# Residual added in PSUM during the expert search, and the expert weight ring reloaded by halves

## The reference, cut to what matters

```python
aff = softmax(h2 @ w_router)                     # 256 tokens x 16 experts
vals, idx = lax.top_k(aff.T, 32)                 # each expert takes its 32 best tokens
xs = h2[idx]                                     # 16 x 32 x 1024
y = (silu(xs @ w_gate) * (xs @ w_up)) @ w_down * vals     # 1024 -> 512 -> 1024
x = x + g_f * zeros.at[idx].add(y)               # back to the tokens' rows
out = rmsnorm(x, norm_final)
```

## Time and profile before

| | us |
|---|---|
| median of 3 runs (lowest, highest) | 679.66 (679.27, 682.19) |
| profiled execution, its own time | 679.7 |
| its span | 677.6 |
| PE busy | 589.6 (87%) |
| DVE busy | 288.5 (43%) |
| ACT busy | 217.5 (32%) |

### The profile page before, as it was taken

How to read it: one execution, slowest core, us unless ns; L and a number is a source line. 1 busy time by engine, 2 the same in 40 slices (tenths; PEclk the granted TensorE clock), 3 DMA queues, 4 the chain that set the end, 5 groups by cost and what they waited for, 6 DMA issues and landing times.

```text
span 677.6 us, 8686 instructions
## 1 busy us (share of the span) xinstructions
PE 589.6 (87%) x3453; PEld 374.9 (55%) x3453; DVE 288.5 (43%) x688; ACT 217.5 (32%) x475; POOL 41.9 (6%) x74
## 2 busy tenths in 40 slices
PE   6989999999998989999999999998999755667554
PEld 6978877778766767748755454457353310121111
DVE  3356576676666350466727877236220100010002
ACT  4245353455334331474426755121010100010001
POOL 3000000000000000100002443000000000000000
PEclk9999999999999998999999999999999898798879
DMA  8594767657688663656568103557899999999994
GB/s 340 191 357 178 302 249 266 264 212 271 260 332 344 242 262 125 249 214 227 196 263 308 66 1 125 231 187 327 340 429 426 428 428 426 427 423 430 428 419 169
DMA packets 19512, 192.48 MB, mean 284 GB/s; under 512 B 3472, under 2 KB 4752, under 8 KB 7696
## 3 DMA queue, kind: packets, MB, share of 16 engines
q1 hardware_dynamic: 16016, 188.49, 69.6%
q10 hardware_dynamic: 3168, 1.87, 1.0%
q0 software_dynamic: 288, 1.57, 0.6%
HBM read 190.35 MB, written 1.05 MB: 282 GB/s over the span
## 4 chain that ended last, share of the span: by engine, by line
PE 64%; DMA 23%; DVE 7%; ACT 3%; issue 2%; POOL 1%; ACTq 0%; SPq 0%; DVEq 0%; POOLq 0%
PE bank L1094 25%; DMA ring<-in_stream 21%; PE bank L1071 6%; PE bank L1082 5%; PE bank L1631 4%; PE bank L1368 3%; PE bank L1581 2%; PE bank L1133 2%; PE bank L1531 2%; PE bank L1499 2%; PE bank L1466 2%; PE bank L1567 2%; PE bank L1422 2%; DMA vvc<-vvc 1%; DVE weight_parts L1912 1%
## 5 line engine op out<-in xcount | busy, mean ns | idle before, releaser
L1094 PE MATMUL bank<-weight_parts,u_parts 128*128 128x512 f32 (+2 forms) x416 | 127.4, 389 | 2.7 <-ACT mo L710 1.1
L1912 DVE TENSOR_TENSOR weight_parts<-ring,weight_parts 128x1024 fp32r<-128x1024 f32 (+2 forms) x64 | 73.2, 1180 | 41.8 <-ACT weight_parts L710 40.0
L1094 PEld LDWEIGHTS bank<-weight_parts,u_parts 128*128 128x128 f32 x416 | 76.7, 191 | 20.8 <-issue 2.6
L710 ACT ACTIVATE weight_parts<-ring 128x1024 fp32r<-128x1024 f32 (+2 forms) x64 | 63.9, 1021 | 34.3 <-PE bank L1094 24.1
L1094 PE MATMUL bank<-weight_parts,x_parts 128*128 128x512 f32 (+1 forms) x128 | 48.4, 378 | 0.0
L1094 PE MATMUL bank<-u_parts,weight_parts 128*128 128x256 f32 x192 | 36.7, 288 | 2.5 <-DVE weight_parts L1912 2.4
L1038 POOL TENSOR_TENSOR small<-small 128x1 f32<-128x1 f32 (+1 forms) x14 | 8.3, 596 | 451.9 <-DVE small L2300 215.6
L774 ACT ACTIVATE sp<-sp,small 128x128 f32<-128x128 f32 (+1 forms) x48 | 21.3, 444 | 36.2 <-DVE small L1836 36.2
L1094 PEld LDWEIGHTS bank<-u_parts,weight_parts 128*128 128x128 f32 x192 | 30.4, 191 | 3.5 <-issue 2.5
L988 ACT ACTIVATE sp<-bank 128x512 f32<-128x512 f32 x4 | 2.4, 597 | 87.5 <-PE bank L1631 87.5
L1631 PE MATMUL bank<-ring,tz 128*32 128x512 f32 x112 | 18.4, 797 | 11.8 <-DMA ring<-in_stream 11.8
(11 more groups left out here) (316 smaller groups left out, 1071.0 us busy)
## 6 DMA issues: line engine op xcount, KB each, us to landing
ring<-in_stream SPq DMA_DIRECT2D x43, 2048.0 KB, 8.9
parts<-in_stream SPq DMA_DIRECT2D x12, 2048.0 KB, 33.5
qk<-in_stream SPq DMA_DIRECT2D x9, 2048.0 KB, 13.2
tabs<-in_stream SPq DMA_DIRECT2D x6, 2048.0 KB, 22.4
mo<-in_stream SPq DMA_DIRECT2D x5, 2048.0 KB, 29.5
vvc<-in_stream SPq DMA_DIRECT2D x5, 2048.0 KB, 32.7
tz<-in_stream SPq DMA_DIRECT2D x5, 1024.0 KB, 37.5
lat<-in_stream SPq DMA_DIRECT2D x5, 1024.0 KB, 39.6
```

The source lines that it names most:

```text
L710: ins = act.activation(dst, src, ACT.Copy, scale=scale)
L1094: ins = pe_.matmul(o, lhs(a, c, i), rhs(b, c, i), start=(c == 0 and n == 0), stop=(c == chunks - 1 and n == 2))
L1912: dve.tensor_tensor(quarter(weight_parts[:, SLOT:], name, q), quarter(slot(name), name, q), quarter(weight_parts, name, q).bitcast(F32), A ...
```

## The change

The residual's four products move from group 0 of the expert loop to the search on DVE, in place of most of the `unread` transposes. `x_sb` is then free, and holds the first half of D0.2. From there on every slot is loaded by halves: the host puts its columns in the order that makes the first half the first 512 columns or the first chunk of all four experts, and each of the 18 half buffers is loaded again when PE has used that half (`h_used`). For group 3, all left halves of D come ahead of all right halves, and the last right half comes in two quarters. The gather of group 0 has a bank for each chunk, DVE and ACT take turns to copy them out, and only the first four chunks stand ahead of G0.0. norm_final is spread in group 1 instead of group 0. At the end the left half of the output is scattered and squared ahead of the right one, with `unread` transposes between the last slots' products; the last right half goes through DVE and the scatter in two quarters of 256 columns, and ACT scales two of the four half rows.

```diff
-WARM = {"ou11": 28, "rT11": 10, "ls1": 8, "afT": 8}
+WARM = {"ou11": 28, "rT11": 10, "ls1": 8}
+WHOLE = 10
+HALVES = ([(name, h) for name in STREAM[N_DENSE + WHOLE:-4] for h in range(2)]
+          + [(f"D{NG - 1}.{i}", h) for h in range(2) for i in range(4)])
+UNITS_IN_RING = 2 * len(EXPERT_CYCLE)
-TAIL = ["ou00", "ou01", "ou10", "rT00", "rT01", "ou11", "rT10", "rT11", "lg1", "ls1", "afT", "slT", "gx0", "gx1"]
+TAIL = ["ou00", "ou01", "ou10", "rT00", "rT01", "ou11", "rT10", "rT11", "lg1", "ls1", "afT", "slT", "gx0", "gx1", "gx2", "gx3",
+        "gx4", "gx5", "gx6", "gx7"]
...
+          **{f"gx{c}": (2, 7, 1)[c % 3] for c in range(KC)}}
...
+        def half_columns(name, half, a, b):
+            if (name, half) not in HALVES:
+                return slot_columns(name, SLOT // 2 * half + a, SLOT // 2 * half + b)
+            k = HALVES.index((name, half))
+            if k == 0:
+                return x_sb[:, a:b]
+            i, h = divmod((k - 1) % UNITS_IN_RING, 2)
+            return slot_columns(STREAM[N_DENSE + i], SLOT // 2 * h + a, SLOT // 2 * h + b)
...
         @block.sync
-            for n, name in enumerate(STREAM):
+            for n, name in enumerate(STREAM[:N_DENSE + WHOLE]):
...
+            for k, (name, h) in enumerate(HALVES):
+                n = STREAM.index(name)
+                if k == 0:
+                    eng.wait_ge(x_added, 1)
+                else:
+                    eng.wait_ge(h_used, k if k <= UNITS_IN_RING else 2 * WHOLE + k - UNITS_IN_RING + 1)
+                w = SLOT // 4 if k == len(HALVES) - 1 else SLOT // 2
+                eng.dma_start(half_columns(name, h, 0, w), stream[n, :, SLOT // 2 * h:SLOT // 2 * h + w])\
+                   .then_inc(half_in(name, h)[0], 16)
+            eng.dma_start(half_columns(name, h, w, 2 * w), stream[n, :, SLOT // 2 + w:]).then_inc(last_quarter, 16)
...
         @block.scalar
+            for t in range(TOK):
+                eng.wait_ge(times_norm, t + 1)
+                eng.wait_ge(roots, 13 + t)
+                act.activation(xn[:, t, 0:512], xn[:, t, 0:512], ACT.Copy, scale=rs[:, 4 + t:5 + t]).then_inc(y_first, 1)
...
         @block.tensor
                 elif name == "slT":
-                    for i in range(CAP // 8):
-                        eng.wait_ge(top_found, i + 1)
-                        unread(WARM["afT"] * (1 + i // 3), bank[3])
+                    eng.wait_ge(x2_ready, 2 * TOK)
+                    for t in range(TOK):
+                        for h in range(2):
+                            ins = pe_.matmul(bank[4 + 2 * t + h][:, :], ident[:, :], xn[:, t, 512 * h:512 * h + 512],
+                                             start=True, stop=False)
+                    ins.then_inc(x_added, 1)
+                    eng.wait_ge(top_found, CAP // 8)
+                    unread(18, bank[3])
...
-            for name in TAIL:
+            for name in TAIL[:-4]:
...
+                        if (g, m) == (0, "G"):
+                            if i in (1, 2):
+                                tail(f"gx{2 * i + 2}")
+                                tail(f"gx{2 * i + 3}")
+                            kept(eng, f"gx{2 * i}")
+                            kept(eng, f"gx{2 * i + 1}")
                         for k in range(2):
+                            half_arrived(eng, f"{m}{g}.{i}", k)
...
-                        ins.then_inc(e_used, 1)
+                            ins.then_inc(h_used, 1)
...
+            g = NG - 1
+            for i in range(4):
+                half_arrived(eng, f"D{g}.{i}", 0)
+                for e in range(EG):
+                    ins = second_products(bank[2], e, i, 0, 0, 512)
+                if i == 3:
+                    ins.then_inc(e_first, 1)
+                unread(9, bank[0])
+            for i in range(4):
+                half_arrived(eng, f"D{g}.{i}", 1)
+                for q, where in ((0, bank[3]), (1, bank[1])):
+                    if (i, q) == (3, 1):
+                        eng.wait_ge(last_quarter, 16)
+                    for e in range(EG):
+                        ins = second_products(where, e, i, 1, 256 * q, 256)
+                    if i == 3:
+                        ins.then_inc(e_quarter, 1)
+                if i == 0:
+                    eng.wait_ge(e_y, NG)
+                    for t in range(TOK):
+                        scattered(g, t, 0).then_inc(e_out, 1)
+                elif i < 3:
+                    unread(9, bank[0])
+            for t in range(TOK):
+                for q in range(2):
+                    if t == 0:
+                        eng.wait_ge(e_y2, NG + q)
+                    ins = scattered(g, t, 1, 256 * q, 256)
+                ins.then_inc(e_out, 1)
...
         @block.vector
-            final_mean(0)
-            eng.wait_ge(roots, n_mean[0] + 1)
-            final_rows(0, 0)
...
+                dve.tensor_tensor(xn[:, t, 0:512], bank[4 + 2 * t][:, :], nfin[:, 0:512], ALU.mult).then_inc(times_norm, 1)
+            for q, where in ((0, bank[3]), (1, bank[1])):
+                a = 256 * q
+                eng.wait_ge(e_quarter, q + 1)
+                dve.tensor_tensor(yE[:, 512 + a:768 + a], where[:, a:a + 256], gF[:, 512 + a:768 + a], ALU.mult)\
+                   .then_inc(e_y2, 1)
+            for t in range(TOK):
+                final_mean(t)
+            for t in range(TOK):
+                eng.wait_ge(roots, n_mean[0] + t + 1)
+                dve.scalar_tensor_tensor(xn[:, t, 512:1024], bank[5 + 2 * t][:, :], rs[:, 4 + t:5 + t], nfin[:, 512:1024],
+                                         ALU.mult, ALU.mult).then_inc(y_ready, 1)
```

More of the change, by code:

```diff
@@ L566, in released @@
                 eng.wait_ge(mod_used, int(name[1:]) + 1)
-            else:
-                group, part = name[1:].split(".")
-                eng.wait_ge(e_used, 12 * int(group) + 4 * "GUD".index(name[0]) + int(part) + 1)
         def experts_done(eng, stage, g):
-            released(eng, f"{stage}{g}.3")
+            eng.wait_ge(h_used, 24 * g + 8 * "GUD".index(stage) + 8)
         def leave(ins, name):
@@ L669, in _ @@
                         filled(eng, "lg1")
[L670 to L676, removed]
+                    eng.dma_start(piece, stream[n, :, i:at]).then_inc(slot_in[b], 16)
                 if name == "W2":
@@ L978, in _ @@
                     soft(1)
-                elif name == "gx0":
+                elif name[:2] == "gx" and int(name[2]) % 2:
                     filled(eng, name)
-                    leave(chosen(D_(name), 0), name)
+                    c = int(name[2])
+                    leave(act.activation(xs[:, c, :], D_(name)[:, 0:P], ACT.Identity,
+                                         bias=mc[:, 0, 24 + c:25 + c], scale=scl[:, 2, c:c + 1]), name)
             for g in range(NG):
@@ L999, in _ @@
                 copy(hT, bank[0][:, :], scale=0.5).then_inc(e_hT, 1)
[L1000 to L1004, removed]
+                if g < 2:
+                    eng.wait_ge(gate_turn, g + 1)
+                    copy((gF, nfin)[g][:, 0:512], bank[0][:, :]).then_inc(gate_a, 1)
             for n, (h, t) in enumerate((h, t) for h in range(2) for t in range(TOK)):
@@ L1556, in tail, with gather @@
                     done(ins, name)
-                elif name in ("gx0", "gx1"):
-                    eng.wait_ge(oh_ready, 1)
+                elif name[:2] == "gx":
+                    if name == "gx0":
+                        eng.wait_ge(oh_ready, 1)
                     begin(name)
[L1560 to L1565, removed]
+                    done(gather(D_(name), 0, [int(name[2])]), name)
+            def gather(o, g, chunks):
+                for i, c in enumerate(chunks):
                     for t in range(TOK):
@@ L1650, in _ @@
                     for i in range(2):
-                        ins = gather(bank[2 + i], g + 1, i)
+                        ins = gather(bank[2 + i], g + 1, range(4 * i, 4 * i + 4))
                     ins.then_inc(side_turn, 1)
@@ L1675, in _ @@
[L1675 to L1681 removed]
+                        ins.then_inc(h_used, 1)
+                    if g < 2 and i == 1:
+                        row = (mc[:, 0, 40:48], nfc)[g]
+                        for c in range(KC):
+                            ins = pe_.matmul(bank[c // 4][:, c % 4 * P:c % 4 * P + P], row[:, c:c + 1].to_broadcast([P, P]),
+                                             ident[:, :], start=True, stop=True)
@@ L1692, in _ @@
-                for h in range(2):
-                    eng.wait_ge((e_y, e_y2)[h], g + 1)
-                    for t in range(TOK):
-                        ins = pe_.matmul(bank[4 + 2 * t + h][:, :], ohT[:, g, t * P:(t + 1) * P],
-                                         yE[:, 512 * h:512 * h + 512], start=False, stop=(g == NG - 1))
-                        if g == NG - 1 or (h, t) == (1, TOK - 1):
-                            ins.then_inc(e_out, 1)
+                            ins = scattered(g, t, h)
```

130 lines of the change are left out of this document (71 added, 59 removed).

## The result

The changed kernel takes 675.49 us (median of 14 executions), the kernel before 682.2 (also of 14): a ratio of 0.9933, with a 95% interval from 0.9915 to 0.9951. So it is faster, by 3.1 to 4.6 us by the ratios, where 7.1 were predicted: 44 to 65% of the forecast gain, with the 675.5 inside the range. The two medians lie 6.7 us apart, but that this is near the forecast is luck: five executions of the kernel before stood at 678.8 to 679.7 and nine at 681.3 to 683.2, and in the second comparison the medians lie 2.7 apart. The changed kernel's executions spread from 674.2 to 678.8. The profiled one took 678.64 (span 676.8), so it is one of the slow end, and that turned out to be the useful thing about it.

A forecast was written before the change was run, and what follows sets the result against it. The weight stream was taken to bound the kernel: restart at 473.45, plus 190.8, -2.45, +1.1 and -0.3 gave the last landing at 662.6; 7.85 for the end and 2.1 over the span gave 672.6 us, range 669.5 to 677.

The forecast's parts named there:

- What bounds the kernel: From 478 to 666 us the weight stream sets the time; its restart, bytes, rate and the work after it count.
- (a): After the dip near 470 us, the first reload of ring goes out at 473.45 instead of 475.94, 2.5 us earlier.
- (b): Half a slot loaded into x_sb during the dip leaves 2.45 us less of stream behind the restart.
- R2: Rival: the half in x_sb brings nothing, as the dip only moves; 675.1 us, chance 0.07.
- (c): In the stream, 34 additional loads cost 1.1 us in all, and finer rows gain 0.3 on the last slot.
- the 418 row: Lowest stream rate of three earlier stretches, 418 GB/s, giving an upper bound of 0.13 us per additional load, 4.4 in all.
- the last slot: At the stream's end, rows of 8 and 4 KB instead of 2 KB take off 0.3 us of a 0.5 us cost.
- R1: Rival: the stream's rate suffers, each additional load costing 0.13 us, in all 4.4; 675.9 us, chance 0.15.
- (d): Behind the last landing, the end takes 7.85 us, 3.0 less, as only a quarter is left to do.
- the 9 transposes behind each piece of D3: Between the last slots' products, 1.12 us with a quad's 0.87 at full clock stays under 2.45 between landings.
- R4: Rival: PE at 1.2 GHz misses the last landings and is about 11 us late; 685.3 us, chance 0.06.
- PE has no idle time before its last loads: Sign at the stream's end that, if seen, would show the forecast to be wrong.

The follow-up runs named there:

- e7: The changed kernel without the transposes in D3 and with nothing loaded into x_sb: 677.09 us, ratio 0.9952 to the kernel before.
- e8: The changed kernel without transposes in D3, nothing in x_sb, and one load per single-buffer slot up to U3.3: 675.5 us, ratio 0.9932 to the kernel before.
- e9: The changed kernel without transposes in D3, with 22 pairs of halves as single loads from the ring's second turn: 673.11 us, ratio 0.9892 to the kernel before.
- e6: The changed kernel without the six batches of transposes in D3, run a second time in another group: 674.65 us, ratio 0.992 to the kernel before.
- e1: The changed kernel without the six batches of nine warming transposes between D3's products: 674.68 us, ratio 0.9914 to the kernel before.
- e10: The changed kernel without transposes in D3, left output halves stored from ACT's queue, right ones from SP's: 675.24 us, ratio 0.9926 to the kernel before.
- e5: The changed kernel itself, measured again in a second comparison: 677.29 us, ratio 0.9955 to the kernel before.
- e4: The changed kernel, transposes kept, nothing in x_sb, and one load per single-buffer slot up to U3.3: 680.3 us, ratio 0.9991 to the kernel before.
- e3: The changed kernel, transposes kept, with nothing loaded into x_sb: 677.45 us, ratio 0.9964 to the kernel before.

## Why the prediction was right or wrong, step by step

**What bounds the kernel** was read rightly: everything that moved the restart, the bytes or the rate moved the end by as much, once PE was on time (e7, e8, e9).

**(a) The restart** came as worked out: 473.45 predicted, 474.06 with 0.6 of delay that was there at the load into tz, ahead of the change. From that load on, the gain is 14.94 - 12.44 = 2.50 us. **(b) The half in x_sb** was worth 2.50 (2.45 predicted), and R2 is refuted by e7.

**(c) The rate was mis-sized.** I took 1.1 us for all additional loads, a quarter of the bound by the 418 row. Measured: from e6 to the kernel before the stretch is 0.37 shorter, with a half of 2.50 left out of it and 0.3 estimated for the last slot, so halves cost 2.4 us (the 0.3 is still the prediction's estimate, no run measured it); e8 says 0.075 and e9 0.09 a slot. The rows that I read held this too weakly: one slot of nine in halves moves a mean of 44 us by 0.1. R1's direction was right, at half its price. Nor did SP's issues cost 0.33 each, as the prediction had it: with many loads queued, single ones held SP for up to 6.30 us in the changed kernel.

```profile
624.39 6.30 SPq L724 DMA_DIRECT2D tz<-in_stream  x1
```

That was hidden all the same: loads issued from 500 to 600 landed 26 to 30 us behind their issue (medians by buffer), and the stream never paused.

**(d) The end was mis-sized.** Behind the landing the engines did what was worked out: squares at L+1.9, the second mean at L+3.5, rows until L+5.1 (5.25 predicted), all in e1. The stores then took 3.7 us instead of 2.6, as all four are ready within 0.8 us and share the transfer (e10), so 8.8 instead of 7.85 and 2.1 us gained instead of 3.0.

**The step that failed** is the one that costs the transposes at nothing: "the 9 transposes behind each piece of D3 cost 1.12 us at full clock, a quad 0.87, together less than 2.45". The slack of 0.35 us at full clock was right. That it covers the transposes was not, for three reasons that the traces show. D3 begins 2.2 us behind its first landing (649.14 against 646.9), which I hadn't worked out at all. The clock is low then: the first half takes 3.98 us (649.14 to 653.12) and the second 3.08, against 2.48. And the first right half carries the scatter as well (2.92). The seven steps from 649.14 to 667.64 take 18.5 us against 17.4 between seven landings. With the 2.2 of the start and 0.43 for the first quarter's pass, which stands ahead of the last quarter's, that makes PE some 3.7 us late. I had the mechanism as R4, but only in its extreme form, at 1.2 GHz all through and 11 us late, with a chance of 6%. Its counter, that PE 80% busy stood at 1.00 from 454 on, didn't hold there: from 640 to 660 PE was busy 17.25 us of 20 at a mean of 0.62. And the prediction named the sign, "PE has no idle time before its last loads", which is what the profile shows. In the profiled execution the last quarter's pass could have begun by about 664.5 (474.06 + 190.45, the stretch of e1 and e6), and it began 0.43 behind 667.64, at 668.1: 3.6 us late. Leaving the batches out brings the waits for loads back (e1, e6) and takes 2.6 us off the median (e5 to e6).

By the Trainium skill (page "TensorE: Matmul & The Clock Gate", section "HAM oscillation — how this bites in real kernels") products that wait for loads start at the low clock again and again. The traces agree: means of 0.62 to 0.83 in the changed kernel's windows from 600 to 660, and the eight passes that start behind a wait at 641.97, and those at 644.46, take 1.93 us, where eight take 1.07 at full clock.

By the Trainium skill (page "DMA: Bandwidth & Descriptors", section "Anatomy of one DMA — SWDGE (gpsimd) path") a DMA has a fixed cost of some 2.0 us, an estimated 68 us for 34 more loads. That section is on DMAs issued by GpSimd, and these are SP's; for loads queued behind each other the runs disagree with the rule as it was used, with 2.4 us for all of them.

The sum with measured terms: -2.5 restart, -2.5 half, +2.4 rate, -0.3 last slot, -2.1 end, +2.6 for PE's lateness, in all -2.4; measured, by the ratios, -3.1 in that group and -4.6 in the first comparison, where the transposes cost 1.3 if e1's ratio, of another group, is set against it. Without the last term it is -5.0, and e6 and e1 have -5.4 and -5.9. Both kernels spread by 3 to 6 us, so which executions a comparison happens to hold moves a ratio by a few tenths of a per cent.

**Open.** What spreads the kernel before over 4 to 6 us, and e8 and e10, which have no transposes, over 4.0 and 5.4; what moves the load into tz, and the restart with it, by up to 1.9 us between executions with the same work ahead (the mean clock up to 460 is 0.99 or 1.00 in every profile); and whether the row's length or the number of loads slows the stream.

## What to carry to other kernels

Where a stream of loads sets the time, warming products between its last pieces need slack at the low clock, not at the full one: PE, which mostly waited for loads here, began that stage at the low clock (0.50 from 640 to 650), and slack of 0.35 us a piece doesn't make up for a start 2.2 us late and 1.5 lost on the first piece. Finer loads are worth having where a buffer's release restarts an idle queue; in the saturated part they cost 0.08 us a slot here, so large rows from the second turn of the ring on gave back 2 us. And time a change at the end of a kernel with the engine on time first, or a true gain can look like a loss (e4 against e3, where e8 against e7 gains 1.6 us).

## What the runs showed of the hardware

- Loads of 1 MB with rows of 8 KB a partition, queued without a gap, moved 421 GB/s from 500 to 640 (changed kernel, e1, e6, e7), loads that are mostly of 2 MB with rows of 16 KB 426 to 427 (before, e8, e9), one execution each.
- PE's clock came back by itself for the end, without any transposes: in e1 it was 0.50 from 640 to 650, 0.95 from 650 to 660 and 1.00 from 660 to 665; it rose while PE worked off the halves that had queued up for D3. In e6 it came later (0.67 from 650 to 660, 0.88 from 660 to 665), and the last product still waited for its load.
- Four stores of 256 KB that become ready within 0.8 us moved 371 to 385 GB/s and ended 3.7 to 3.8 us behind the last row, with one issuing queue (e1) or two (e10); with the rows ready over 2.1 us it was 2.45 (before).
- With many loads of 1 MB queued, one issue held SP for up to 6.30 us (changed kernel, at 624.39), while the DMA engines stayed busy (share 1.01 from 620 to 640).
